# Sums of weight blocks in four gated down projections: from VectorE to accumulating DMAs issued by GpSimd

## The reference, cut to what matters

```python
def swiglu(x, w_in, w_out):
    gate, up = jnp.split(x @ w_in, 2, axis=-1)
    return (jax.nn.silu(gate) * up) @ w_out
```

## Time and profile before

| | |
|---|---|
| device time, median of 3 runs | 2822.73 us |
| span of the profiled execution | 2818.6 us |
| its own device time | not recorded apart; the median of the runs is 4.1 us above the span |
| PE busy | 2765.8 us, 98% |
| DVE busy | 1955.9 us, 69% |
| ACT busy | 1384.3 us, 49% |
| POOL busy | 58.2 us, 2% |
| mean granted TensorE clock | 0.998 |
| share of the 16 DMA engines (SP's queue) | 26.9% |

### The profile page before, as it was taken

How to read it: one execution, slowest core, us unless ns; L and a number is a source line. 1 busy time by engine, 2 the same in 40 slices (tenths; PEclk the granted TensorE clock), 3 DMA queues, 4 the chain that set the end, 5 groups by cost and what they waited for, 6 DMA issues and landing times. The chain is left out here.

```text
span 2818.6 us, 48303 instructions
## 1 busy us (share of the span) xinstructions
PE 2765.8 (98%) x19892; PEld 2464.4 (87%) x19892; DVE 1955.9 (69%) x2715; ACT 1384.3 (49%) x2115; POOL 58.2 (2%) x45
## 2 busy tenths in 40 slices
PE   8999999999999999999999999999999999999998
PEld 7999888788999888999888778999888889888887
DVE  7887855676887876887855677788774469655541
ACT  4445544554544465544544555444555366444430
POOL 1000000001000001000000000100000000000000
PEclk9999999999999999999999999999999999999999
DMA  4334311103234241334222103233432211323331
GB/s 149 106 105 172 103 48 63 37 3 120 84 106 138 101 135 53 105 105 175 69 77 68 47 3 113 75 105 106 150 104 84 75 35 34 112 80 96 97 124 53
DMA packets 71065, 254.77 MB, mean 90 GB/s; under 512 B 7672, under 2 KB 8696, under 8 KB 70848
## 3 DMA queue, kind: packets, MB, share of 16 engines
q1 hardware_dynamic: 70848, 251.70, 26.9%
HBM read 249.57 MB, written 2.10 MB: 89 GB/s over the span
## 5 line engine op out<-in xcount | busy, mean ns | idle before, releaser
L261 PE MATMUL ps<-h_hi,w_space 128*128 128x512 f32 (+1 forms) x2624 | 697.2, 351 | 3.4 <-DVE h_lo L359 3.4
L271 PE MATMUL ps<-w_space 128*128 128x512 f32 x2448 | 567.3, 390 | 1.3 <-PEq L91 0.8
L271 PEld LDWEIGHTS ps<-w_space 128*128 128x128 f32 x2448 | 457.4, 188 | 96.1 <-issue 1.2
L261 PEld LDWEIGHTS ps<-h_hi,w_space 128*128 128x128 f32 x2624 | 462.4, 190 | 69.4 <-DVE h_lo L359 4.2
L249 DVE TENSOR_TENSOR w_space<-w_raw,w_space 128x1024 fp32r<-128x1024 f32 x256 | 311.9, 1231 | 258.7 <-ACT w_space L241 258.4
L261 PE MATMUL ps<-h_lo,w_space 128*128 128x512 f32 (+1 forms) x1312 | 456.9, 348 | 0.0
L942 PE MATMUL ps<-h_hi,w_space 128*128 128x256 f32 x2432 | 450.8, 283 | 0.0
L942 PEld LDWEIGHTS ps<-h_hi,w_space 128*128 128x128 f32 x2432 | 385.1, 192 | 0.2
L241 ACT CAST w_space<-w_raw 128x1024 fp32r<-128x1024 f32 x256 | 264.8, 1047 | 187.9 <-PE ps L261 102.9
L942 PE MATMUL ps<-h_lo,w_space 128*128 128x256 f32 x1216 | 344.1, 283 | 0.0
L261 PEld LDWEIGHTS ps<-h_lo,w_space 128*128 128x128 f32 x1312 | 249.3, 190 | 30.3 <-issue 0.5
(11 more groups left out here) (471 smaller groups left out, 3868.6 us busy)
## 6 DMA issues: line engine op xcount, KB each, us to landing
w_raw<-in_w_ffn_in SPq DMA_DIRECT2D x176, 512.0 KB, 3.7
w_raw<-in_w_in SPq DMA_DIRECT2D x64, 512.0 KB, 3.7
w_raw<-in_w_ffn_out SPq DMA_DIRECT2D x56, 512.0 KB, 3.7
w_raw<-in_w_up SPq DMA_DIRECT2D x44, 512.0 KB, 3.7
row_blocks<-in_w_ffn_out SPq DMA_DIRECT2D x8, 2048.0 KB, 11.8
w_raw<-in_w_out SPq DMA_DIRECT2D x24, 512.0 KB, 4.1
w_raw<-in_w_down SPq DMA_DIRECT2D x22, 512.0 KB, 3.7
w_raw<-in_w_ple_gate SPq DMA_DIRECT2D x16, 512.0 KB, 4.1
```

Of the source, the lines that this page charges most:

```text
L261: m = nc.tensor.matmul(c.ps[:, bank, t], part[:, cols], moving[:, k, t], start=(opens and k == 0 and i == 0), stop=(k == KD - 1 and i == 2 ...
L271: m = nc.tensor.matmul(c.ps[:, bank + half, :], x, part[:, half * S:(half + 1) * S], start=(first and i == 0), stop=(final and i == 2), sk ...
```

## The change

The four weight sums of each group are no longer made by DVE. GpSimd issues, for each, a DMA that reads one 512 KB block (128 partitions x 2 x 512 float32) from the weights in HBM and adds it to a block that stands in `row_blocks`. [...] So the signs in the method are turned: m5 uses b11 + b12, m6 adds b22 to it, m7 is b12 + b22, and m4 adds b21 to m6's. The activation sums and the ways in which the products are combined get the signs that fit.

GpSimd waits before each DMA for the block to be loaded (or for the sum before it in the same group) and for the `lo` of the unit that used the block last. The semaphore `blocks_summed` of the group tells ACT that a sum is there; before, this was `seven_rested` of DVE. Four semaphores elsewhere are merged, with the same instructions waiting on the same ones.

```diff
@@ waiting
             if name in SUMMED_WEIGHTS:
-                self.wait_rested(eng, "weights", name, g)
+                self.wait_summed(eng, name, g)
...
+    def wait_summed(self, eng, name, g):
+        eng.wait_ge(self.c.blocks_summed[g], 16 * (len(SUMMED_WEIGHTS) * self.stage + SUMMED_WEIGHTS.index(name) + 1))
...
+    def gpsimd_down(self, pool, nc):
+
+        c = self.c
+        places = {"b11": (0, 0), "b12": (0, 1), "b21": (2, 0), "b22": (2, 1)}
+        sums = {"m5": ("b11", "b12", "m1"), "m6": ("b11", "b22", "m5"), "m7": ("b12", "b22", "m6"), "m4": ("b11", "b21", "m6")}
+        for name in SUMMED_WEIGHTS:
+            into, added, last_use = sums[name]
+            for g in range(2):
+                if name == "m5":
+                    self.wait_blocks(pool, g)
+                else:
+                    self.wait_summed(pool, SUMMED_WEIGHTS[SUMMED_WEIGHTS.index(name) - 1], g)
+                pool.wait_ge(c.W.lo_ready, self.down.d0 + STEP_OF[last_use, g] + 1)
+                (row, half), (added_row, added_half) = places[into], places[added]
+                nc.gpsimd.dma_start(c.row_blocks[:, g, row:row + 2, half * S:(half + 1) * S],
+                                    self.w_blocks[g][:, added_row:added_row + 2, added_half * S:(added_half + 1) * S],
+                                    accum_op=ALU.add).then_inc(c.blocks_summed[g], 16)
...
@@ vector_down
             self.collect(dve, nc, k)
-            if k + 2 < UNITS and DOWN_STEPS[k + 2][0] in SUMMED_WEIGHTS:
-                self.weight_sum(dve, nc, *DOWN_STEPS[k + 2])
             if k + 1 < UNITS and DOWN_STEPS[k + 1][0] in SUMMED_ACTS:
                 self.act_sum(dve, nc, *DOWN_STEPS[k + 1])
...
@@ act_sum
-            nc.vector.tensor_tensor(total, a21, a22, ALU.add).then_inc(done, 1)
+            nc.vector.tensor_tensor(total, a21, a22, ALU.subtract).then_inc(done, 1)
         if name == "m6":
-            nc.vector.tensor_tensor(total, total, a11, ALU.subtract).then_inc(done, 1)
+            nc.vector.tensor_tensor(total, a11, total, ALU.subtract).then_inc(done, 1)
```

More of the change, by code:

```diff
@@ L554, in scalar_tables @@
         c = self.c
-        act.wait_ge(c.reduced, 1)
+        act.wait_ge(c.table_chain, 8)
         nc.scalar.activation(c.rope[:, 1, :], c.ang, ACT.Sin).then_inc(c.sines, 1)
@@ L741, in __init__ @@
             rested += self.collected(k)
-            rested += [("weights",) + step for step in DOWN_STEPS[k + 2:k + 3] if step[0] in SUMMED_WEIGHTS]
             rested += [("acts",) + step for step in DOWN_STEPS[k + 1:k + 2] if step[0] in SUMMED_ACTS]
@@ L1320, in take_out, with combine, join @@
                                 ALU.subtract).then_inc(c.seven_rested, 1)
[L1322 to L1326, removed]
+    def combine(self, dve, nc, one, other, op, into):
+        nc.vector.tensor_tensor(self.block_sum(into), self.block_sum(one), self.block_sum(other), op).then_inc(self.c.seven_rested, 1)
+    def join(self, dve, nc, name, product, op):
         banks = self.block_banks(name)
-        nc.vector.tensor_tensor(banks, banks, self.block_sum(product), ALU.add).then_inc(self.c.seven_rested, 1)
+        nc.vector.tensor_tensor(banks, banks, self.block_sum(product), op).then_inc(self.c.seven_rested, 1)
     def collect(self, dve, nc, k):
@@ L1343, in collect @@
             self.wait_rested(dve, "out", "m7")
-            self.add_sums(dve, nc, "m6", "m7")
+            self.combine(dve, nc, "m6", "m7", ALU.add, "m7")
         if k == STEP_OF["row", TAKEN["m7"]] + 4:
             dve.wait_ge(c.W.done, self.down.d0 + STEP_OF["row", TAKEN["m7"]] + 1)
-            self.join(dve, nc, "m7", "m6")
+            self.join(dve, nc, "m7", "m6", ALU.add)
             self.wait_rested(dve, "three", "m1", "m6", "m7")
-            self.join(dve, nc, "m5", "m7")
+            self.join(dve, nc, "m5", "m7", ALU.subtract)
         if k == STEP_OF["m3", 1] + 4:
             dve.wait_ge(c.W.done, self.down.d0 + STEP_OF["m3", 1] + 1)
-            self.join(dve, nc, "m6", "m5")
+            self.join(dve, nc, "m6", "m5", ALU.add)
 class Proj(Up):
@@ L3219, in rotate @@
         if t == 0:
-            dve.wait_ge(c.table_loaded, 16)
+            dve.wait_ge(c.positions_loaded, 48)
         if t >= 2:
@@ L3918, in _ @@
                 ffn.gpsimd(pool, nc)
+                ffn.gpsimd_down(pool, nc)
                 attention.gpsimd(pool, nc)
@@ L3970, in _ @@
                 if table is not None:
-                    sp.dma_start(c.rope[:, :, :], table).then_inc(c.table_loaded, 16)
+                    sp.dma_start(c.rope[:, :, :], table).then_inc(c.positions_loaded, 16)
                 if ffn1 is not None:
@@ L3982, in _ @@
                 if table is not None:
-                    sp.wait_ge(c.table_loaded, 16)
+                    sp.wait_ge(c.positions_loaded, 48)
             @block.gpsimd
@@ L3988, in _ @@
                 ffn2.gpsimd(pool, nc)
+                ffn2.gpsimd_down(pool, nc)
                 if ffn1 is not None:
                     ffn1.gpsimd(pool, nc)
+                    ffn1.gpsimd_down(pool, nc)
                     attention.gpsimd(pool, nc)
@@ L4152, in signals @@
     c.rows_loaded = [sem(f"rows_loaded{n}") for n in range(NT)]
+    c.blocks_summed = [sem(f"blocks_summed{g}") for g in range(2)]
     c.ident_loaded, c.positions_loaded, c.consts_loaded = sem("ident_loaded"), sem("positions_loaded"), sem("consts_loaded")
     c.rec_loaded = sem("rec_loaded")
-    c.made, c.reduced, c.sines, c.table_chain, c.table_loaded = (sem(n) for n in ("made", "reduced", "sines", "table_chain", "table_loaded"))
+    c.made, c.sines, c.table_chain = (sem(n) for n in ("made", "sines", "table_chain"))
     c.y_done, c.y_split, c.y_ready = sem("y_done"), sem("y_split"), sem("y_ready")
```

18 lines of the change are left out of this document (3 added, 15 removed).

## The result

| | before | changed |
|---|---|---|
| device time, median of 7 runs each (lowest to highest) | 2822.91 us (2820.18 to 2823.90) | 2829.97 us (2826.50 to 2834.45) |
| ratio to before, 95% interval | | 1.0027 [1.0016, 1.0038] |
| span of the profiled execution | 2818.6 us | 2827.1 us |
| its own device time | not recorded apart | 2828.92 us |

The changed kernel is slower by 7.1 us in the medians, and by 0.27% by the ratio of the table. The time lies in the range of the prediction, but not in its likeliest case. That case was no measurable change, at 2823.7. What came is rival 1, which had put its first point, T = 9 on idle engines and 11 beside a load, at 2830. The ratio's lower end, 1.0016, leaves open whether the loss is a little under 0.2%; it is not zero.

The account below looks back on a forecast made before the run. PE's matmul stream was taken as the bound. Profiled span 2818.6 plus 4.1 to the median made 2822.7; removed work counted 0, added waits 1.0, so 2823.7 us, with a range of 2819 to 2842.

Parts of the forecast that it names:

- rival 1: First sum of each FFN: slow adding DMA holds ACT, the copy and PE; 2830 to 2851; chance 0.27 beyond T = 8.5.
- T: Time from when GpSimd may issue an adding DMA until its sum has landed; forecast 5.4 us on idle DMA engines.
- What bounds the kernel: Four down projections: PE busy 348.00 of 348 us, so removing 39.0 us of DVE sums is worth 0.
- Rivals 3 and 4: 3: DVE was a hidden pacemaker, faster, 2820.9, chance 0.06. 4: DVE follows ACT, nothing moves, 2822.7, within the forecast's 0.67.
- The place: First sum of each FFN, m5 of g0, is tight: ACT's cast of unit 7, then the copy PE needs before step 4.
- room: Largest T before PE waits at step 4: 6.8, 9.5, 8.4 and 9.8 us in the four FFNs; later sums have more.
- GpSimd's own part: In T: nothing counted for GpSimd's work in issuing, 0.1 us for the handover.
- The first FFN: Second block lands at 259.4, with the gate at 259.1: nothing to share, so T 5.4 against 6.8 us.
- The load beside it: Third FFN: even sharing with the second 2 MB block, T 6.8 to 7.2; about 7 in second and fourth.
- The bytes: In T: an adding DMA reads both operands, 1 MB, at 3.3 us per MB plus a fixed 2.0 us.
- Rival 2: Stolen bandwidth delays unit 5 of the second group; 2824.4 at most; shares the 0.67 for no measurable change.
- The 4.1 us: Whole program before the change: added to the profiled span of 2818.6 to reach the median, 2822.7.

Follow-up runs that it names:

- Experiment 1: Changed kernel with all 32 sums left out on every engine, products using unsummed blocks, against the kernel before: ratio 0.9998, 2820.48 us.
- experiments 3: Changed kernel with only the 8 sums of m5 as adding DMAs, the other 24 back on DVE, against the kernel before: ratio 1.0032, 2830.74 us.
- experiment 4: Changed kernel with m5 of g0 (4 of 32 sums) back on DVE, the other 28 by DMA, against the kernel before: ratio 1.0006, 2823.70 us.
- experiment 7: Changed kernel with the same 32 DMAs copying instead of adding, against the kernel before: ratio 0.9999, 2821.10 us.
- experiment 2: Changed kernel with the 8 sums of m5 back on DVE, the other 24 by adding DMA, against the kernel before: ratio 1.0003, 2821.81 us.
- experiments 6: Changed kernel with ACT's first copy ahead of unit 7's cast and DVE's take-out of m1 at round 7, against the kernel before: ratio 1.0030, 2830.39 us.
- experiment 10: Changed kernel with m5, m6, m4 built in b12's place and a fifth, copying DMA per group, against the kernel before: ratio 1.0057, 2837.23 us.
- experiment 9: Changed kernel with the DMA for m5 of g0 waiting for unit 5's `lo` instead of unit 4's, against the kernel before: ratio 1.0091, 2847.07 us.
- experiment 5: Changed kernel with ACT's first copy out of PSUM ahead of the cast of unit 7, against the kernel before: ratio 1.0015, 2825.85 us.

## Why the prediction was right or wrong

**What bounds the kernel: right.** PE was the bound, and DVE's 39 us (34.6 measured as busy time) are worth nothing. Experiment 1 shows it by itself. Rivals 3 and 4 fall: nothing got faster, and something moved.

**The place: right.** The first sum of each FFN holds ACT's cast, this the copy, this PE at step 4; the sums behind it have room. The tests for it were experiments 3 and 4. The prediction's own subtraction gives the sum of the waits once the measured T is put in: 8.25 - 6.8, 10.67 - 9.5, 10.29 - 8.4 and 10.71 - 9.8 make 1.45, 1.2, 1.9 and 0.9, 5.4 in all. PE waited for 1.22, 1.45, 1.14 and 1.92, 5.7. That the sums agree so well is in part luck, since the single terms are off by up to 1.0. (The room of the third FFN comes out at 8.5, not 8.4: 1338.69 less 2.08 is 1336.6.)

**The step that failed: T.** It was taken as 5.4 on idle engines, the first FFN among them, and as 6.8 to 7.2 beside the load. Measured are 6.5 to 7.5 with least beside it (m6 of g0), 8.25 in the first FFN, and 10.3 to 10.7 beside the load. The term was mis-sized in three pieces; a fourth, the bytes, was near.

*GpSimd's own part.* I wrote that nothing was in it for issuing and had 0.1 for the handover. Measured: 0.55 to 0.65 us from the gate to the start of the issue, and 1.2 us of issuing, and none of this lies beside the transfer. The first adding DMA of experiment 4 is issued from 263.79 to 265.12, with the engines mostly free. From 263.79 to 265.80 not one packet of GpSimd's queue q0 moves, only packets of SP's:

```profile
q1 hardware_dynamic: 62, 0.18, 22.3%
```

A copying DMA of GpSimd lands in 4.5 us (median; 4.0 at the least), where SP's load of the same size had taken 3.7. "DMA: Bandwidth & Descriptors" ("Anatomy of one DMA — SWDGE (gpsimd) path"), also of the Trainium skill, would give about 3.2 us for 512 KB as an estimate. Counted from the start of the issue, as the landings here are, the measurement decides against it; from the end of the issue, the shortest copy is near it (4.0 - 0.7 = 3.3), so what the estimate lacks is GpSimd's issue.

*The first FFN.* The prediction had "nothing to share" there, because the second block lands with the gate. But SP's loads of 512 KB follow that block, and in the kernel before they keep the engines full until 262, 2.9 us past the gate (1.03 is the DMA share):

```profile
259.00:262.00 3.00, 3.00 (x15) 2.49 (x14) 1.65 (x3) 2.52 (x3) 0.00 (x0) 1.00 1.03 422
```

In the changed kernel the sum of m5 of g1 comes on top. T is 1.7 us longer than that of m6 of g0 in the same FFN, and this piece decides there: 6.5 would still have been under the room of 6.8.

*The load beside it.* Mine was 1.4 to 1.8 us more, by even sharing with a block that is then 1.3 to 2.5 us late. It is 3.2 to 4.2 more than m6 of g0 in the same FFN, and the sharing isn't even. In the second FFN the issue ends at 923.49 (922.28 + 1.21), and until 926.70 all packets are those of q1:

```profile
q1 hardware_dynamic: 340, 1.25, 103.1%
```

The second blocks land from 1.2 us sooner after their issue (third FFN) to 1.1 us later (fourth) than before; the median of all eight loads is 12.0 instead of 11.8.

*The bytes: near.* 3.3 us per MB made 1.6 us for the 0.5 MB more that an adding DMA was taken to read. Adding cost 1.8 (5.9 against 4.1, experiment 7), 0.48 of it GpSimd's issue. The engines' time, 3.6% of the span for 32 sums or 3.2 us each, against 1.7% or 1.5 us each for copies, fits two reads. The Trainium skill has the same factor in "Collectives: The Full Stack" ("The bandwidth ceiling: the fold count and why AG ≠ RS ≠ AR"): half the rate of a copy. That it comes from two reads is not shown here, since the number of packets doubles as well.

The prediction had both ends, 3.7 and 11.8, and chose the lower "because the bytes are" nearer. T lay in between them, and the room of 6.8 us was a quarter above the chosen value, on engines that were not idle. With the likeliest value so near the point of decision, and every piece that was left out able only to add time, rival 1 deserved more than 0.27. Its price was right: 7.5 us of waits forecast for T = 9 and 11, 5.7 measured for 8.25 and 10.6.

**Rival 2 falls.** The second block is hardly late, and the traffic costs PE nothing by itself: 24 of the 32 DMAs (experiment 2) and the copying DMAs, which take less than half of the engines' time of the adding ones (experiment 7), leave the time where it was. Plain loads do get slower, 4.8 us instead of 3.7, but they have room.

**The 4.1 us** between the profiled span and the median were in part the spread of the runs: in every one of the changed kernel's runs the device time lies 1.8 to 1.9 us above its span, so that the profiled execution of before was a quick one. The forecast's absolute value hardly moves by this, since it is anchored on the median.

**Open.** What the median holds beyond the waits in experiments 6 (2.7 us) and 10 (over 7 us). Why an adding DMA holds the engines twice as long: two reads or twice the packets. A version in which the copy has a place outside ACT's queue wasn't tried. Of all versions run, none is faster than the kernel before; by experiment 1 there was next to nothing to gain.

## What to carry to other kernels

Where the bounding engine has no wait, work taken from another engine is worth nothing, and the only question left is what the replacement's latency does: here 1.2 us on DVE became 6.5 us from gate to use with little beside it, 8 with other DMAs under way and over 10 beside a 2 MB load. So count the room of each sum singly, against the DMA share of the window in which it will run and not against an idle queue: one of eight had too little, and moving that one back removed the waits. Moving an instruction past a late one on an in-order queue mostly hands the wait on to the next queue (ACT, then DVE, then the next take-out), and early data is what removes it.

## What the runs showed of the hardware

- A long PE wait had a price of its own, in the granted clock. After waits of 1.14 to 1.92 us the next 24 matmuls took 5.69 to 5.73 us instead of 5.60, at a granted clock of 1.00. After 3.10 to 4.87 us they took 7.08 to 8.57, with means of 0.65 to 0.80 over them (experiment 9), and after 2.36 us 12 matmuls took 4.39 instead of 3.01, at 0.66 (experiment 5). At 2.1 us both were seen (experiment 10: a wait of 2.13 in the second FFN with 5.69 us at 1.00 behind it, and 2.08 in the fourth with 7.29 us at 0.77).
- An adding DMA of GpSimd occupied the DMA engines for 2.1 times as long as the same DMA that copies (3.6% against 1.7%), in 272 packets instead of 144 (8704 and 4608 for 32), and GpSimd for 1.20 us instead of 0.72.
- GpSimd's issue and the transfer didn't overlap: with the engines mostly free, the first packet moved 0.7 us behind the end of the issue (experiment 4). Beside a full queue of SP it took 3.2 us (changed kernel, second FFN).
- Two such DMAs released by one event are issued one behind the other, 2.58 us for the pair:

```profile
263.41 2.58 POOL L948 DMA_DIRECT2D row_blocks<-in_w_ffn_out  x2 [224.04 <-DVE w_space L249]
```

No issue of an adding DMA of 512 KB took less than 1.19 us in these runs, so a row of such sums on GpSimd follows at that pace at best.
